# Expert stage: heads of both tiles in turn, one query a block, and eight gather slots from the start

## The reference

```
q  = (x @ w_q)                          # [128 tokens, 8 heads, 2 halves, 128]
s  = q . keys                           # [128, 8, 2, 128]
top 16 of each half -> 256 sums -> top 16 -> 16 expert numbers, gate = softmax
a  = x . u[expert];  w = gate * gelu(a)
y += w * v[expert]                      # 8 heads x 16 experts a token
```

## Time and profile before

| | |
|---|---|
| median of 3 runs | 4465.04 us (4461.28 to 4473.89) |
| the profiled execution's own time | 4468.27 us |
| its span | 4466.4 us |
| TensorE busy | 3671.1 us, 82% |
| VectorE busy | 2783.9 us, 62% |
| ScalarE busy | 1611.4 us, 36% |
| gather queue's share of the 16 DMA engines | 74.7% |
| HBM read | 1569.69 MB |

### The profile page before, as it was taken

The page is one execution under the profiler, slowest core; times in us unless marked ns, Lnnn a source line. Parts: engine busy times, 40 slices in busy tenths (PEclk is TensorE's granted clock), DMA queues, the critical chain, the costliest instruction groups (busy, mean ns, idle before and its releaser), DMA issues.

```text
span 4466.4 us, 40877 instructions
## 1 busy us (share of the span) xinstructions
PE 3671.1 (82%) x10990; PEld 1671.0 (37%) x10990; DVE 2783.9 (62%) x6988; ACT 1611.4 (36%) x4770; POOL 1414.6 (32%) x1337
## 2 busy tenths in 40 slices
PE   5997988788888778897987778988887778897877
PEld 2444454223443222344542223444422224442222
DVE  2227656777766677446666775456677755666775
ACT  0123234444444444332344443123444431444443
POOL 0000234444344444201344442003444431344432
PEclk7988999999999999999999999999999999999999
DMA  5335599999999999864999998649999995999998
GB/s 230 143 121 201 237 395 404 421 421 420 414 418 419 415 412 415 341 234 189 385 401 421 421 421 358 245 188 380 405 421 421 420 375 203 373 406 421 420 421 333
DMA packets 207495, 1573.63 MB, mean 352 GB/s; under 512 B 23104, under 2 KB 23232, under 8 KB 30624
## 3 DMA queue, kind: packets, MB, share of 16 engines
q0 software_dynamic: 191952, 1370.57, 74.7%
q1 hardware_dynamic: 15120, 200.26, 11.5%
q10 hardware_dynamic: 192, 0.20, 0.0%
HBM read 1569.69 MB, written 1.25 MB: 352 GB/s over the span
## 4 chain that ended last, share of the span: by engine, by line
DMA 46%; PE 34%; DVE 10%; ACT 4%; issue 3%; DVEq 1%; POOL 1%; ACTq 0%; SPq 0%; POOLq 0%
DMA arena<-uv,idx 45%; PE banks L1016 14%; PE banks L551 8%; DVE arena L2075 5%; PE banks L669 4%; PE banks L584 2%; ACT diag L1302 1%; PE banks L565 1%; DMA weight_ring<-weights 1%; ACT wgt L1300 1%; POOL arena L498 1%; ACT gel L1298 1%; PE banks L850 1%; PE banks L738 0%; PE banks L537 0%
## 5 line engine op out<-in xcount | busy, mean ns | idle before, releaser
L1016 PE MATMUL banks<-arena,diag 128*128 128x512 f32 x5120 | 2512.1, 625 | 626.0 <-ACT diag L1302 624.0
L2075 DVE CUSTOM_DVE_ANT_0 arena<-arena 128x1024 f32<-128x1024 f32 x1280 | 1567.7, 1225 | 920.3 <-DMA arena<-uv,idx 910.2
L498 POOL DMA_INDIRECT arena<-uv,idx x1280 | 1385.5, 1082 | 2366.9 <-PE banks L1016 1826.8
L1016 PEld LDWEIGHTS banks<-arena,diag 128*128 128x128 f32 x5120 | 921.5, 194 | 2131.0 <-ACT diag L1302 1361.4
L1298 ACT ACTIVATE gel<-dot 128x1 f32<-128x1 f32 x1280 | 258.6, 202 | 1681.4 <-DVE dot L2075 1680.2
L1302 ACT ACTIVATE diag<-consts_sb,wgt 128x128 f32<-128x128 f32 x1280 | 514.0, 402 | 92.0 <-issue 5.1
L1300 ACT ACTIVATE wgt<-gel,gate 128x1 f32<-128x1 f32 x1280 | 376.9, 294 | 90.7 <-issue 3.5
L551 PE MATMUL banks<-weight_ring,arena 128*128 128x512 f32 (+2 forms) x908 | 386.7, 585 | 5.3 <-DVE hidden_sb L1585 1.8
L551 PEld LDWEIGHTS banks<-weight_ring,arena 128*128 128x128 f32 x908 | 172.8, 192 | 208.2 <-issue 195.6
L669 PE MATMUL banks<-arena,weight_ring 128*128 128x256 f32 (+1 forms) x1152 | 233.0, 356 | 0.0
L669 PEld LDWEIGHTS banks<-arena,weight_ring 128*128 128x128 f32 x1152 | 200.6, 190 | 52.3 <-issue 30.6
(11 more groups left out here) (253 smaller groups left out, 2296.0 us busy)
## 6 DMA issues: line engine op xcount, KB each, us to landing
weight_ring<-weights SPq DMA_DIRECT2D x75, 2048.0 KB, 8.9
arena<-weights SPq DMA_DIRECT2D x12, 2048.0 KB, 10.0
arena<-uv,idx POOLq DMA_INDIRECT x1280, 15.2
row_ring<-mods POOLq DMA_DIRECT2D x34, 512.0 KB, 14.3
row_ring<-gains POOLq DMA_DIRECT2D x18, 512.0 KB, 14.5
arena<-keys SPq DMA_DIRECT2D x4, 1024.0 KB, 13.8
weight_ring<-weights SPq DMA_DIRECT2D x2, 1536.0 KB, 12.3
arena<-weights SPq DMA_DIRECT2D x3, 1024.0 KB, 7.2
```

What stands on the lines that cost most here:

```text
L498: pool.indirect_dma_start(out=ring[:, RING_SLOT[k], :], out_offset=None, in_=A[f"uv{l}"], in_offset=bass.IndirectOffsetOnAxis(ap=idx[:, UN ...
L1016: ins = mm_(bank[:, yb, :], diag[:, s, :], ring[:, s, D + hf * 512:D + hf * 512 + 512], start=first, stop=last, skip_group_check=True)
L2075: sig(V.tensor_tensor_reduce(out=ring[:, s, 0:D], in0=ring[:, s, 0:D], in1=xnat_of(u[0], u[1]), scale=1.0, scalar=0.0, op0=ALU.mult, op1=A ...
```

## The change

The units of a layer go in a new order that takes both tiles in turn (`ORDER`). Every query is made for one tile and one head (128 columns), three units ahead, in every unit; queries keep the room of two units (512 columns in place of 2048) and scores the room of four (1024 in place of 4096). The ring grows down into that room and has eight slots at all times; X0 lies behind it, X1 under its slots 6 and 7. The first gather into slot 0 of a layer waits for the last output projection. Blocks for x0 no longer wait for the last sum; the last block of query weights goes to x0, and some blocks change places. The input of layer 0's second round is made tile by tile, beside units 8 and 12, and the end of a layer's first tile lies beside its last four units. In the differential attention the two reciprocals go to a place of their own, the factor of the second map is joined into one number a token, one pass makes p0 + factor * p1, and the first map's reciprocal is applied in ScalarE's copy of the head's output.

```diff
-FIRST_SLOTS, FIRST_UNITS = 6, 4
-PE_BESIDE = {0: (10, 11, 14, 15), 1: (2, 4, 7, 9, 11, 13), 2: (2, 4, 7, 9, 11, 13), 3: (2, 4, 7, 9, 11, 13), None: (2, 7, 11, 13)}
-ACT_BESIDE = {0: (12, 13, 15), 1: (4, 6, 9, 11, 13, 15), 2: (4, 6, 9, 11, 13, 15), 3: (4, 6, 9, 11, 13, 15), None: (4, 9, 13, 15)}
+ORDER = ((0, 0), (0, 1), (0, 2), (0, 3), (1, 0), (0, 4), (1, 1), (0, 5), (1, 2), (0, 6), (1, 3), (0, 7), (1, 4), (1, 5), (1, 6), (1, 7))
+PE_BESIDE = {0: (2, 5, 8, 12, 13), None: (2, 7, 11, 13, 14)}
+ACT_BESIDE = {0: (3, 6, 9, 13, 14), None: (4, 9, 12, 13, 15)}
-    return [(r, i, h) for r in ROUNDS_OF[l] for i in range(2) for h in range(PH)]
+    return [(r, i, h) for r in ROUNDS_OF[l] for i, h in ORDER]
...
+            k = first + n
+            slot.append((k + 2) % SLOTS)
+            use.append(k // SLOTS + 1)
+            before.append(k - SLOTS if n >= SLOTS else None)
...
-SCORES = QT + 8 * 2 * P
-KEYS = SCORES + 2 * PH * 2 * NK
-RING = KEYS + 2 * PH * NK
-ARENA = RING + SLOTS * 2 * D
+SCORES = QT + 4 * P
+KEYS = SCORES + 4 * 2 * NK
+RING = 9216
+X1 = RING + 6 * 2 * D
+X0 = RING + SLOTS * 2 * D
+ARENA = X0 + 4096
...
-    out += queries(0, "x0", 0, 1, 0) + queries(1, 1, 0, 1, 0)
-    out += block(1, 1, "kv") + mods(2, 0, 0) + block("x0", 1, "q0") + block("x1", 1, "q1")
+    out += queries(0, "x0", 0, 1, "x0") + queries(1, 0, 1, "x0", 0)
+    out += block(1, 1, "kv") + block("x0", 1, "q0") + mods(2, 0, 0) + block("x1", 1, "q1")
...
-                if where in ("x0", "x1"):
+                if where == "x1":
                     l = name[0] - (name[1] == "mod")
-                    if l:
-                        sp.wait_ge(*after("sum", slot_at(units_of(l - 1)[-1], TOPK - 1)))
-                    else:
-                        sp.wait_ge(*after("mix", 0, 3))
+                    sp.wait_ge(*after("sum", slot_at(units_of(l - 1)[-1], TOPK - 1)))
+                if where == "x0" and name[0] == 0:
+                    sp.wait_ge(*after("mix", 0, 3))
...
-                        elif RING_SLOT[k] == FIRST_SLOTS:
-                            pool.wait_ge(*after("w", BLOCK_AT[(l, "wq", 0, ROUNDS_OF[l][0])]))
+                        elif RING_SLOT[k] == 0:
+                            pool.wait_ge(*after("mm", l, "out1", 3, 0))
...
+                def query(u):
+                    r, i, h = u
+                    t, m = ROUNDS[r][1][i], UNIT_AT[u] % 2
+                    if (r, t) not in queried:
+                        queried.add((r, t))
+                        pe.wait_ge(*after("ev", r, "xT2", t, 0))
+                        pe.wait_ge(*after("ev", r, "xT2", t, 1))
+                    for hp in (2 * h, 2 * h + 1):
+                        j, c = divmod(hp, 4)
+                        n, w = weights((l, "wq", j, r), KC)
+                        b = new_bank(r, "q", hp, i)
+                        for kk in range(KC):
+                            ins = mm_(bank[:, b, 0:P], w[:, kk, c * P:(c + 1) * P], xT2[:, kk, i * P:(i + 1) * P],
+                                      start=kk == 0, stop=kk == KC - 1)
+                        over = i == 1 and c == 3
+                        ins.then_inc(sems["pe"], done("pe", ("mm", r, "q", hp, i), *([("w", n)] if over else [])))
+                        yield
...
+                    beside = query(units[n + 3]) if n + 3 < len(units) else iter(())
                     if n == 0:
-                        beside = chain(peer_input(r0, ROUNDS[r0][1][1:]), beside)
+                        beside = chain(beside, peer_input(r0, ROUNDS[r0][1][1:]))
+                    if l == 0 and n in (11, 14):
+                        beside = chain(beside, peer_input(1, LAT[:1] if n == 11 else LAT[1:]))
...
+                if n >= 4:
+                    act.wait_ge(*after("idx", *UNITS[n - 4]))
+                ev(a.copy(scores[:, n % 4, :], bank[:, b, 0:256]), r, "sc", h, i)
...
-                            ev(a.copy(v3(MIX, 4, D)[:, t, 512 + h * P:512 + (h + 1) * P], bank[:, b, 0:P]), 0, "O", i)
+                            c = 8 * (i % 4) + 6
+                            ev(AF(v3(MIX, 4, D)[:, t, 512 + h * P:512 + (h + 1) * P], bank[:, b, 0:P], ACT.Copy, scale=small[:, c:c + 1]),
+                               0, "O", i)
...
-                            V.reciprocal(small[:, c + 2:c + 4], small[:, c + 2:c + 4])
+                            V.reciprocal(small[:, c + 6:c + 8], small[:, c + 2:c + 4])
                             dve.drain()
-                            V.tensor_scalar(pr1, pr1, small[:, c + 3:c + 4], lamc[:, 3:4], ALU.mult, ALU.mult)
+                            V.scalar_tensor_tensor(out=small[:, c + 3:c + 4], in0=small[:, c + 2:c + 3], scalar=small[:, c + 7:c + 8],
+                                                   in1=lamc[:, 3:4], op0=ALU.mult, op1=ALU.mult)
                             dve.drain()
-                            sig(V.scalar_tensor_tensor(out=pr0, in0=pr0, scalar=small[:, c + 2:c + 3], in1=pr1, op0=ALU.mult,
+                            sig(V.scalar_tensor_tensor(out=pr0, in0=pr1, scalar=small[:, c + 3:c + 4], in1=pr0, op0=ALU.mult,
                                                        op1=ALU.add), ("Pr", 0, i))
...
+                    tail = n - len(units) + 16
+                    if n == 1:
+                        run(peer_input(r0, (tb,)))
+                    if l == 0 and n in (12, 15):
+                        run(peer_input(1, LAT[:1] if n == 12 else LAT[1:]))
...
-                    if u == (ROUNDS_OF[l][-1], 1, 0):
+                    if tail == 12:
                         between = end_of_layer(l, 2)
...
-                        if j == 5 and h == 0 and n:
-                            before = units[n - 1]
-                            run(peer_residual(before[0], before[1]))
+                        if j == 5 and n and units[n - 1][2] == PH - 1:
+                            run(peer_residual(*units[n - 1][:2]))
```

More of the change, by code:

```diff
@@ L75, in ring_plan @@
 def ring_plan():
-    slot, use, before, count = [], [], [], [0] * SLOTS
+    slot, use, before = [], [], []
     for l in range(LAYERS):
-        order, last = list(range(FIRST_SLOTS)), {}
+        first = len(slot)
         for n in range(len(units_of(l)) * TOPK):
-            if n == FIRST_UNITS * TOPK:
-                order = list(range(FIRST_SLOTS, SLOTS)) + order
-            s = order.pop(0)
-            order.append(s)
-            count[s] += 1
-            slot.append(s)
-            use.append(count[s])
-            before.append(last.get(s))
-            last[s] = len(slot) - 1
+            k = first + n
+            slot.append((k + 2) % SLOTS)
+            use.append(k // SLOTS + 1)
+            before.append(k - SLOTS if n >= SLOTS else None)
     return slot, use, before
@@ L124 @@
 WCOLS = 4096
-X0, X1 = (RING + 2048 * n for n in (6, 4))
 GATES = 27680
@@ L677, in query_head @@
                         pe.wait_ge(keys_landed, 16 * (l + 1))
[L678 removed]
+                    b = new_bank(r, "sc", h, i)
                     for q in range(2):
[L680 to L685 removed]
@@ L686, in query_head @@
-                    ins.then_inc(sems["pe"], done("pe", ("mm", r, "sc", h, *key)))
+                        pe.wait_ge(*after("ev", r, "q", 2 * h + q, i))
+                        ins = mm_(bank[:, b, q * P:(q + 1) * P], qT[:, 2 * m + q, :], keys_sb[:, 2 * h + q, :], start=True, stop=True)
+                    ins.then_inc(sems["pe"], done("pe", ("mm", r, "sc", h, i)))
                     yield
                 def lead(t):
-                    return chain(peer_input(r0, (t,)), query_head(r0, 0, 0), query_head(r0, 1, 0))
+                    return chain(peer_input(r0, (t,)), query(units[0]), query(units[1]))
@@ L999, in _ @@
                         pass
-                for _ in query_head(r0, 2, 0):
+                for _ in query(units[2]):
                     pass
@@ L1309, in _ @@
                 exps(units[1])
-                for _ in take_head(r0, 2, 0):
+                for _ in take(units[2]):
                     pass
@@ L2102, in _ @@
                         beside = iter(())
-                    if u == (0, 1, 0):
-                        between = modulated(l, LAT, 0, ("g2", "sc2", "sh2"), [xnat_of(1, q) for q in range(2)], "xnat", norm)
-                    if u == (0, 1, 4):
-                        beside = chain(peer_input(1, LAT), beside)
+                    tail = n - len(units) + 16
[3 more added lines that the diff above has]
+                        run(peer_input(1, LAT[:1] if n == 12 else LAT[1:]))
+                    if l == 0 and n in (8, 12):
+                        t = 2 if n == 8 else 3
+                        rows_ = [row(0, name, 0) for name in ("g2", "sc2", "sh2")]
+                        between = tile_input(0, t, xnat_of(1, t - 2), rows_, norm, t == 2,
+                                             [("xnat", 0, t)] + ([("row", m) for m, _ in rows_] if t == 3 else []))
                     if l < 2 and u == (l + 1, 0, 0):
```

(2 more changed lines are left out.)

107 lines of the change are left out of this document (33 added, 74 removed).

## The result

| | before | after |
|---|---|---|
| median, us | 4465.34 (4461.28 to 4473.89, 4 runs) | 4421.54 (4416.81 to 4422.27, 4 runs) |
| span of the profiled execution | 4466.4 | 4419.9 |

A forecast was written before the change was run, and what follows sets the result against it. Gather DMA was taken to bound the expert stages, with sum stalls losing time in each layer's first five units. Terms -48 + 12.5 - 3.5 = -39 us gave 4429, or 4426 as median; range 4400 to 4457.

The forecast's parts named there:

- The 77 us: First 5 units of each layer: DMA moves less than the full 421 GB/s, together 77.3 us lost.
- slack of 4.3 and 9.3 us: Gather ring: a stall under 4.3 us is free with six slots, under 9.3 with eight.
- -48 us for this term: First five units: eight slots and narrow, moved queries win three quarters of 65 us; bounds 65 and 25.
- the 65 that were to be had: Of 77.3 us DMA loss, 12 at the layer starts (3 us each) stay, so 65 can be won.
- +12.5 us for weights in full stages: Expert stages: x0 weights loaded ahead cost their bytes at 421 GB/s, 5.0 twice and 2.5; bounds 0 and +12.5.
- 0 for the end work: Tile 2's end work, now in units 12 to 14 instead of 8 to 13, fits: 0, bounds -2 and +6.
- -3.5 us for the differential maps: Differential attention: 16 passes become single-column ones of about 0.17 us, VectorE saves 5.0; bounds 0 and -5.0.
- narrow queries at nothing: TensorE in expert units: narrow queries add 10.8 us but lie beside gathers in 7.8 us idle a unit; cost nothing.
- the slower rival: All expert units: 40 new query units each lose one expert's 2.49 us, +61 in all, 4526 us; chance 0.09.
- the VectorE case: Unit 0: VectorE's lag holds, only 25 us come, 4449 us, chance 0.18; with end work's +6 it set the range's 4457.
- the forecast's own rival at 4398: First five units: all the loss goes and the weights hide, 4398 us; chance 0.10.
- The signs: Expected: 410 GB/s or more early, eight gathers running; wrong if later units fall under 421 or fronts change over 5 us.

The follow-up runs named there:

- the last experiment: Changed kernel with the x0 mixer blocks of the next layer and three more weight blocks (5.8 MB) held until the stage's last sum: 4396.8 us, ratio 0.9831.

## Why the prediction was right, step by step

**Right: what lost the DMA time and what cures it.** The 77 us were stalls of TensorE's sums that a ring of six does not bear. Under a load matched to that of the kernel before, two slots more take 49.7 of them (77.2 to 27.5) and 48.5 us of time (4481.5 to 4433.0). The even load takes 39.3 (77.2 to 37.9) with six slots and 13.5 with eight. The parts do not add up: either hides most of what the other hides, and that is why undoing slots and position made it look as if the slots were worth a third. Moving the early query is, with eight slots, worth 10 us of idle time under load (27.5 to 17.3) and nothing without. The prediction's slack of 4.3 and 9.3 us for six and eight slots has the right order: the pause of 6.86 us lies between them. As a threshold it is too sharp, since unit 1 of layer 2 still loses 4.4 us with eight. The load was matched with narrow products in the changed kernel; the wide form itself, with its waits on ScalarE and VectorE, was not put back alone.

**Mis-sized: -48 us for this term.** Measured -62.9 of the 65 that were to be had. I held a quarter back for VectorE in unit 0 and for new waits; unit 0 did keep its lag, but the ring carries much of it (layer 2's unit 0 runs at 370 GB/s with six slots and the change's positions, 2966 to 3012 us there, and at 399 with eight), and in layers 1 and 2 the whole first stretch loses 2.0 us, less than the 3 us that I gave up as lost at each start.

**Right: +12.5 us for weights in full stages.** 11.4 us of stage by the account of the stretches, and -15 us when the same blocks wait again. This was the largest cost of the change and it was avoidable.

**Mis-sized: 0 for the end work.** The later stretches lost 8.5 us more, over the bound of +6. In layers 1 to 3 it stands where the second tile's end work now shares the last units with queries, top-k and norms. Layer 2 of the changed kernel, with one of POOL's waits, and then the same units of the kernel at 4481 us (six slots at the start, more load there), which has the same end work:

```profile
3493.00:3513.00 20.00, 16.73 (x47) 7.89 (x46) 17.58 (x39) 7.38 (x25) 8.16 (x8) 0.91 0.97 381
3513.00:3533.00 20.00, 13.87 (x29) 5.47 (x28) 14.80 (x42) 9.36 (x26) 7.54 (x7) 0.83 0.99 407
3533.00:3553.00 20.00, 17.29 (x39) 6.50 (x37) 16.33 (x42) 6.54 (x23) 12.00 (x10) 1.00 1.00 401
...
3503.57 1.16 POOL L493 DMA_INDIRECT arena<-uv,idx  x1 [5.56 <-PE banks L1005]
```

```profile
3533.00:3553.00 20.00, 16.96 (x50) 8.49 (x51) 16.52 (x35) 6.84 (x23) 7.45 (x8) 0.91 1.01 422
3553.00:3573.00 20.00, 13.64 (x31) 5.26 (x29) 16.04 (x46) 9.18 (x26) 9.91 (x8) 1.00 1.01 418
3573.00:3593.00 20.00, 15.23 (x31) 5.23 (x31) 15.68 (x39) 7.04 (x24) 10.07 (x9) 1.00 1.01 422
```

1.9, 0.7 and 1.0 us are lost in the changed kernel (20 us less 20 x g/421), with VectorE 17.58 of 20 us busy in the first. The other kernel loses next to nothing in the same units, and its later stretches lose 50.1 us in all, near the 48.5 of the kernel before and not the 57.0 of the changed one. With eight slots and the load they lose 51.2 us with the late query and 56.8 with the early one. So the place of the end work alone does not make the loss; what it has to meet with stays open. The busy time of a whole stretch (231 of 308) could not have shown it either way.

**Mis-sized: -3.5 us for the differential maps.** The section got 2.3 us shorter and the kernel not measurably. The new small pass takes 0.22 us and not the 0.17 assumed. The front of layer 0 came out 8.1 us shorter than in the one profile of the kernel before, which would have looked like a confirmation; but over the 13 kernels run with the change or a part of it it scatters from 481 to 490 us, with old maps 485. What makes the 493 of the kernel before stays open.

**Right for a wrong reason: narrow queries at nothing.** They are hidden, at 0.123 us each. But the room is 11.3 us a unit, not 7.8, and the slower rival (every unit carries a query, 4526 us) was further off than its chance of 0.09: three times the products in 68 of the 80 queries cost 7 us by the medians and nothing by the ratios. The queries' own 17.2 us, against 10.8 forecast, did not show either.

In sum: -62.9 + 11.4 + 8.5 in the stages, and -3.4 in the fronts that no experiment could pin down, is -46.4, against -46.5 of the two spans and -39 forecast. The error of -15 in the first term was met by +8.5 in the end work and +3.5 of maps that did not show, less 1.1 of weights and these fronts. That 4426 came within 5 us of 4421.5 is in part luck. The range was not a clean sum either: the VectorE case with the end work's +6 is 4455, not 4457, and the lower end of 4400 lies above the forecast's own rival at 4398. Nothing hangs on either.

**The signs.** Five held: 410, 417, 417 and 411 GB/s in the first five units, eight gathers in a row, the gap of 8.34 us gone, the wide form gone (the narrow one at 0.123 us, not 0.119), L1818's pass gone. Two that were named as signs of being wrong appeared: the later stretches run at 414, 410, 409 and 410 GB/s where the kernel before has 414, 412, 412 and 412, and are 11, 10, 11 and 2 us longer; and the front of layer 0 is 8.1 us shorter, over the 5 allowed.

## What to carry to other kernels

In a loop that DMA sets, slots and an even load are two cures for the same stall: price them together, and test each with the other undone, or the first to be removed looks cheap. Count the slack as slots x transfer less one trip, and compare it with the longest pause, pauses that follow closely taken together, not with the mean load. Do not load ahead into a stage whose DMA is full: 11.0 MB cost 24 us of stage there, while the fronts of layers 1 to 3 of these kernels use about half of their DMA (share 0.45 to 0.52).

## What was not expected of the hardware

TensorE at 97% busy (38.76 of 40 us) kept pace with a full DMA, since its sums took 0.446 us in a row and 0.495 behind a wait; idle time understated its room by 3.5 us in 40.

With three times the queries the granted clock was higher: 0.955 of full speed over the span in the changed kernel at 83% busy, 0.971 at 90% (0.952 to 0.957 and 0.969 to 0.974 over their runs). Busy time alone does not order it, since the kernel before has 0.963 at 82%. In two steady units of layer 2 it is 1.00 and 0.96 at 34.44 and 34.58 us busy, and in three of the other kernel 1.00 each, at 38.76 to 39.44. What the higher clock saved is not shown.

The front of layer 1 took 214 us at clock 0.97 in the changed kernel and 220 at 0.93 in the last experiment, with weight waits of 1.7 and 1.3 us: single profiles of a front can differ by more than many an edit is worth.
